# A fused transformer kernel in which both double norms and the first norm get their steps in another order

## The reference

```
def rmsnorm(x, g):
    y = x * rsqrt(mean(x * x, axis=-1) + EPS)
    return y * g

def first_block(x, ...):
    for i in range(2):
        h = rmsnorm(x, norm_mix[i])                 # n0, n2
        x = x + (forgetting_attention, retention)[i](h, ...)
        h = rmsnorm(x, norm_ffn[i])                 # n1, n3
        x = x + swiglu(h, ffn_w_in[i], ffn_w_out[i])
    return rmsnorm(x, final_norm)                   # fin

def second_block(x, ...):
    for i in range(2):
        u = rmsnorm(x, norm_pre[i])                 # n4, n5
        y = (nsa_mixer, diff_mixer)[i](u, ...)
        x = x + rmsnorm(y, norm_post[i])            # post0, post1
    return x
```

## Time and profile before

| | us |
|---|---|
| median of 3 runs | 2117.72 (2117.28 to 2118.42) |
| the profiled execution, its own time | 2117.17 |
| its span | 2115.9 |
| TensorE busy | 2051.3 (97%) |
| VectorE busy | 965.9 (46%) |
| ScalarE busy | 779.4 (37%) |
| GpSimd busy | 323.0 (15%) |

### The profile page before, as it was taken

One profiled execution on the slowest core, in us unless ns is written; L12 is line 12 of the kernel. 1 busy time (PEld: TensorE's weight loads), 2 busy tenths in 40 slices (PEclk: granted clock), 3 DMA queues, 4 the chain that ended last, 5 costly groups with the idle time before them and its releaser, 6 DMA issues. The chain is left out here.

```text
span 2115.9 us, 26709 instructions
## 1 busy us (share of the span) xinstructions
PE 2051.3 (97%) x10149; PEld 1659.6 (78%) x10149; DVE 965.9 (46%) x1967; ACT 779.4 (37%) x1557; POOL 323.0 (15%) x489
## 2 busy tenths in 40 slices
PE   7999999999999999999999999989998999899998
PEld 5887887888888886788888888867787888677766
DVE  4438434433354344435524444354435663535445
ACT  4226332222233222332322222233336884324453
POOL 2103110000002120000110000032003764402311
PEclk9999999999999999999999999999999999999999
DMA  5330232332324331132233333225321102323212
GB/s 175 101 91 19 60 123 89 92 99 90 101 69 149 100 91 50 51 99 100 79 121 91 98 100 93 90 72 181 99 70 61 32 22 100 103 80 100 70 50 80
DMA packets 96766, 187.32 MB, mean 89 GB/s; under 512 B 8407, under 2 KB 16639, under 8 KB 96512
## 3 DMA queue, kind: packets, MB, share of 16 engines
q1 hardware_dynamic: 90288, 164.35, 25.5%
q0 software_dynamic: 6352, 21.27, 3.2%
HBM read 181.33 MB, written 4.26 MB: 88 GB/s over the span
## 5 line engine op out<-in xcount | busy, mean ns | idle before, releaser
L1902 DVE TENSOR_TENSOR wl<-raw,wh 128x1024 fp32r<-128x1024 f32 x306 | 375.8, 1234 | 782.0 <-ACT wh L1352 781.1
L1352 ACT ACTIVATE wh<-raw 128x1024 fp32r<-128x1024 f32 x306 | 320.8, 1053 | 833.4 <-PE bank L729 796.8
L729 PE MATMUL bank<-hTh,wh 128*128 128x512 f32 (+2 forms) x1200 | 467.5, 390 | 0.2 <-issue 0.2
L729 PE MATMUL bank<-hTl,wh 128*128 128x512 f32 (+2 forms) x1200 | 466.9, 389 | 0.0
L729 PE MATMUL bank<-hTh,wl 128*128 128x512 f32 (+2 forms) x1200 | 466.9, 389 | 0.0
L729 PEld LDWEIGHTS bank<-hTh,wh 128*128 128x128 f32 (+2 forms) x1200 | 223.9, 187 | 48.7 <-issue 0.3
L729 PEld LDWEIGHTS bank<-hTh,wl 128*128 128x128 f32 (+2 forms) x1200 | 223.9, 187 | 48.1
L729 PEld LDWEIGHTS bank<-hTl,wh 128*128 128x128 f32 (+2 forms) x1200 | 223.9, 187 | 48.0
L729 PE MATMUL bank<-wh,hTh 128*128 128x512 f32 x400 | 156.5, 391 | 0.1
L729 PE MATMUL bank<-wh,hTl 128*128 128x512 f32 x400 | 155.7, 389 | 0.0
L729 PE MATMUL bank<-wl,hTh 128*128 128x512 f32 x400 | 155.6, 389 | 0.0
(11 more groups left out here) (368 smaller groups left out, 3105.4 us busy)
## 6 DMA issues: line engine op xcount, KB each, us to landing
raw<-in_ffn_w_in SPq DMA_DIRECT2D x88, 512.0 KB, 3.6
raw<-in_ret_w_in SPq DMA_DIRECT2D x48, 512.0 KB, 3.8
raw<-in_ffn_w_out SPq DMA_DIRECT2D x44, 512.0 KB, 3.7
raw<-in_diff_w_in SPq DMA_DIRECT2D x32, 512.0 KB, 3.7
raw<-in_fox_w_in SPq DMA_DIRECT2D x24, 512.0 KB, 3.9
raw<-in_nsa_w_in SPq DMA_DIRECT2D x20, 512.0 KB, 3.6
raw<-in_ret_w_out SPq DMA_DIRECT2D x16, 512.0 KB, 3.7
raw<-in_fox_w_out SPq DMA_DIRECT2D x8, 512.0 KB, 3.7
```

The source lines that it names most:

```text
L729: i = pe.do.matmul(dst, x, y, start=first and k == 0 and q == 0, stop=stop)
L1352: act.do.activation(M.hl[n % HL_SLOTS][0][:, 0:m], M.raw[n % RAW_SLOTS][:, 0:m], ACT.Copy).then_inc(*T.up("act_hi", n))
L1902: dve.do.tensor_tensor(wl[:, 0:m], M.raw[n % RAW_SLOTS][:, 0:m], wh[:, 0:m].bitcast(F32), ALU.subtract).then_inc(*T.up("dve_lo", n))
```

## The change

1. **SP's queue at the start:** x tile 0, gain, chunk 0, x tile 1, chunks 1, 2 and 3, x tiles 2 and 3, then the rest as before.
2. **The gain of n0** is multiplied by -0.5 by VectorE, no longer by ScalarE.
3. **ScalarE and VectorE at the start:** ScalarE splits chunk 0 between the squares of tiles 0 and 1 and chunk 1 ahead of turn 0; VectorE does the splits of chunks 0 and 1 ahead of turn 0, and scale 1 behind turn 0 and one more split.
4. **TensorE at the double norms:** D0 D1 D2 turn 0, D3, V0 with turn 1 in its middle (`turn_at=2`), V1 with turn 2 in its middle, V2 with turn 3, V3. The other norms name their turns by tile now, with the same order as before.
5. **ScalarE and VectorE at the double norms:** `act_between`, `act_final` and `dve_between` go; `act_double` and `dve_double` write the whole order out.

The number of instructions of each kind is the same, except that the one multiply of the gain moves from ScalarE to VectorE. GpSimd's program is unchanged.

```diff
+    load_x(0)
     sp.do.dma_start(M.norm["n0"][0][:, :], M.I["norm_mix"][0]...)
-    load_x(0)
+    load_weights(0)
     load_x(1)
-    load_weights(0)
-    load_weights(1)
+    for n in (1, 2, 3):
+        load_weights(n)
     load_x(2)
-    load_weights(2)
     load_x(3)
...
-                if c == 3 and late:
+                if c == turn_at and late:
...
-    pe_ffn(pe, T, M, 1, ("n3", {2: (3,)}), ("n4", 2))
+    pe_ffn(pe, T, M, 1, ("n3", {2: (3,)}), ("n4", {2: (0,)}))
...
-    pe_by_tile(pe, T, M, ["nsa v"], ..., late=("n4", {1: (2,), 2: (3,)}))
+    pe_by_tile(pe, T, M, ["nsa v"], ..., late=("n4", {0: (1,), 1: (2,), 2: (3,)}),
+               turn_at=2)
...
 def act_program(act, T, M):
-    gain = M.norm["n0"][0]
-    act.wait_ge(*T.at("ldn0", "gain"))
-    act.do.activation(gain[:, :], gain[:, :], ACT.Copy, scale=-0.5)...
...
     squares(0)
+    act_split(act, T, M)
     squares(1)
     act_split(act, T, M)
     act_turn(act, T, M, "n0", 0)
-    for _ in range(3):
-        act_split(act, T, M)
+    act_split(act, T, M)
+    act_split(act, T, M)
     squares(2)
...
+def act_double(act, T, M, post, norm, first, rest=None):
...
+    first(0)
+    rest_of(0)
+    squares(0)
+    first(1)
+    rest_of(1)
+    first(2)
+    act_turn(act, T, M, norm, 0)
+    squares(1)
+    act_split(act, T, M)
+    rest_of(2)
+    act_split(act, T, M)
+    act_split(act, T, M)
+    first(3)
+    act_turn(act, T, M, norm, 1)
+    squares(2)
+    rest_of(3)
+    act_split(act, T, M)
+    act_turn(act, T, M, norm, 2)
+    squares(3)
...
 def dve_program(dve, T, M):
-    dve_scale(dve, T, M, "n0", 0, "act_gain")
+    dve.wait_ge(*T.at("ldn0", "gain"))
+    dve.do.tensor_scalar(gain[:, :], gain[:, :], -0.5, None, ALU.mult)...
+    dve_scale(dve, T, M, "n0", 0, "dve_gain")
...
+def dve_double(dve, T, M, post, norm, first, rest):
...
+    taken(0)
+    rest(0)
+    dve_whole(dve, T, M, post, 0)
+    taken(1)
+    rest(1)
+    taken(2)
+    dve_scale(dve, T, M, norm, 0, "pool_gain")
+    dve_whole(dve, T, M, post, 1)
+    dve_turn(dve, T, M, norm, 0)
+    rest(2)
+    taken(3)
+    dve_split(dve, T, M)
+    dve_split(dve, T, M)
+    dve_scale(dve, T, M, norm, 1, "pool_gain")
+    dve_whole(dve, T, M, post, 2)
+    dve_split(dve, T, M)
+    rest(3)
+    dve_turn(dve, T, M, norm, 1)
+    dve_scale(dve, T, M, norm, 2, "pool_gain")
+    dve_whole(dve, T, M, post, 3)
+    dve_split(dve, T, M)
+    dve_turn(dve, T, M, norm, 2)
+    dve_scale(dve, T, M, norm, 3, "pool_gain")
```

More of the change, by code:

```diff
@@ L773, in pe_by_tile @@
         if closes:
-            norm, lag = closes
-            if o >= lag:
-                pe_turn(pe, T, M, norm, o - lag)
+            norm, tiles = closes
+            for t in tiles.get(o, ()):
+                pe_turn(pe, T, M, norm, t)
 def pe_by_half(pe, T, M, tag, ready, freed, late):
@@ L1547, in act_ffn, with both, final, squares @@
         a, b = (act_add_and_turn(act, T, M, "n2", f"down05 {half}", half) for half in range(2))
[L1548 to L1576 removed]
+        def both(o):
+            a(o)
+            b(o)
+        act_by_tile(act, T, M, both)
+    else:
+        def final(half):
+            return lambda t: act_squares(act, T, M, "fin", t, half, M.X[:, t, half * 512:half * 512 + 512], "dve_x", (f"down15 {half}", t))
+        act_double(act, T, M, "fin", "n4", final(0), final(1))
+    T.note("act", f"ffn{i}")
+def act_double(act, T, M, post, norm, first, rest=None):
+    def squares(t):
+        for half in range(2):
+            act_squares(act, T, M, norm, t, half, M.X[:, t, half * 512:half * 512 + 512], "dve_x", (post, t))
+    def rest_of(t):
+        if rest:
+            rest(t)
+    first(0)
[17 more added lines that the diff above has]
+    squares(3)
 def act_ret(act, T, M):
@@ L1650, in act_nsa @@
     bank = T.bank
[L1651 removed]
+    act_by_tile(act, T, M, late=("n4", {0: (3,)}))
     def take_c(o):
@@ L1917, in dve_product, with dve_by_tile @@
         dve_split(dve, T, M)
-def dve_by_tile(dve, T, M, take=None, late=None, before_last=None):
+def dve_by_tile(dve, T, M, take=None, late=None):
     for o in range(4):
@@ L2165, in dve_ffn, with both, taken @@
         a, b = (dve_add_and_scale(dve, T, M, "n2", f"down05 {half}", half) for half in range(2))
-    else:
-        a, add = (dve_add(dve, T, M, f"down15 {half}", half) for half in range(2))
-        def b(o):
-            add(o)
-            dve_between(dve, T, M, "fin", "n4", o)
-    def both(o):
-        a(o)
-        b(o)
-    dve_by_tile(dve, T, M, both, before_last=(lambda: dve_scale(dve, T, M, "n4", 2, "pool_gain")) if i else None)
-    T.note("dve", f"ffn{i}")
-def dve_between(dve, T, M, post, norm, o):
-    if o == 3:
-        while dve.held:
-            dve_release(dve, T, M)
-    if o >= 2:
-        dve_turn(dve, T, M, norm, o - 2)
-    if o in (1, 2):
-        dve_scale(dve, T, M, norm, o - 1, "pool_gain")
-    dve_whole(dve, T, M, post, o)
-    if o == 3:
-        dve_scale(dve, T, M, norm, 3, "pool_gain")
+        def both(o):
+            a(o)
+            b(o)
+        dve_by_tile(dve, T, M, both)
+    else:
+        dve_double(dve, T, M, "fin", "n4", *(dve_add(dve, T, M, f"down15 {half}", half) for half in range(2)))
+    T.note("dve", f"ffn{i}")
+def dve_double(dve, T, M, post, norm, first, rest):
+    def taken(t):
+        if first:
+            first(t)
+    taken(0)
[10 more added lines that the diff above has]
+    dve_split(dve, T, M)
+    dve_split(dve, T, M)
+    dve_scale(dve, T, M, norm, 1, "pool_gain")
+    dve_whole(dve, T, M, post, 2)
+    dve_split(dve, T, M)
+    rest(3)
+    dve_turn(dve, T, M, norm, 1)
+    dve_scale(dve, T, M, norm, 2, "pool_gain")
+    dve_whole(dve, T, M, post, 3)
+    dve_split(dve, T, M)
+    dve_turn(dve, T, M, norm, 2)
+    dve_scale(dve, T, M, norm, 3, "pool_gain")
 def dve_whole(dve, T, M, post, o):
```

64 lines of the change are left out of this document (19 added, 45 removed).

## The result

| | before | after |
|---|---|---|
| median of 4 runs each, side by side, us | 2117.93 (2117.28 to 2118.42) | 2101.98 (2100.59 to 2103.39) |
| profiled execution: own time / span, us | 2117.17 / 2115.9 | 2103.34 / 2102.0 |

The ratio is 0.9925 (95%: 0.9908 to 0.9942), so the kernel became 16 us faster. The forecast was 2102.5, range 2099 to 2109.

A forecast was written before the change was run, and what follows sets the result against it. TensorE, 97% busy, was taken as the bound, so only its waits and slow-clock time could be won. 8.0 + 5.1 + 2.1 = 15.2 us off 2117.17 gives 2102.0, plus 0.55 for the median: 2102.5, range 2099 to 2109.

The forecast's parts named there:

- nothing downstream should eat it: Outside the changed stages: TensorE is full, splits and transfers follow its releases, so the summed 15.2 us stay won.
- fin/n4: First double norm: V0 right behind D3, one 2.2 us wait before its last chunk; 8.0 us less, bounds 7.0 and 9.5.
- The favourable rival: Both double norms: GpSimd gets in between splits, outer norm 2 and split 3 come 1 to 2 us earlier; 2099, chance 0.13.
- post0/n5: Second double norm: same order and prices, a 2.1 us wait, V2 starts earlier; 5.1 us less, bounds 4.1 and 6.8.
- The start: Kernel start: first product's matmul at 14.7 instead of 16.85; 2.1 us less, 1.1 to 2.9 depending on the clock.
- the 2.9 of the working: Kernel start: the case that the clock rises 3.4 us earlier, making the start worth 2.9 us.
- The clock did not fall in the new waits: Rival, both double norms: clock falls in the 2.2 us waits, 2.4 us each; 2105 or 2107.3, chance 0.27.
- The roots did not starve VectorE: Rival, double norms: roots caught twice by VectorE instructions, 10.5 us later per stage; 2123.5, chance 0.04.
- VectorE held by GpSimd: Rival, double norms: VectorE waits for GpSimd's running step, 1.5 us per stage, 3 us; 2105.5, chance 0.03.

The follow-up runs named there:

- swap: The changed kernel with VectorE's split 3 ahead of outer norm 2 instead of behind it, in both double norms; 2102.62 us, ratio 0.993.
- gain_act: The changed kernel with the gain's multiply back on ScalarE, ahead of the squares; 2101.80 us in one execution.
- orders_only: The kernel before with only ScalarE and VectorE in the new order at the double norms, TensorE and start as before; 2103.30 us, ratio 0.9929.
- roots: The changed kernel with GpSimd's roots reordered in both double norms, outer norm 2's root before VectorE's splits 1 and 2; 2102.70 us, ratio 0.9928.
- best: The changed kernel with roots reordered in both double norms, fin 2's sum made earlier, and turn 0 ahead of split 1 at the start; 2097.06 us, ratio 0.9906.

## Why the prediction was right, point by point

The time was right (2101.98 for 2102.5), and so were the mechanisms of all three terms. That it came within 0.5 us is luck: two errors of opposite sign cancelled. The three terms were set too small by 3.1 us, and the step "nothing downstream should eat it" failed by 4.6 us in the profiled execution.

- **fin/n4: 9.2 us, predicted 8.0 (bounds 7.0 to 9.5).** The mechanism was the predicted one: V0 right behind D3, one wait for low halves ahead of its last chunk. What was mis-sized is the chain of roots. Against D0's start scale 1 came 1.0 us earlier than in the working (1412.56 with a lead of -0.27, for 1413.3), so that turn 1 had no wait instead of 0.5; outer norm 2 came 1.2 us earlier (1415.55 for 1416.5), and the wait was 1.08 us instead of 2.2. Most of this comes from further up the chain. The working had every GpSimd step beside scale 0 wait for its end, but the first step of the root of fin 1 was over before scale 0 began (1403.20 to 1403.49), the second took its 0.56 us beside it, and only the third was held up (1404.24, 0.81 us). So outer norm 1 started at 1405.50 (1405.2 against D0's start, for 1406.1), the squares of n4 1 and ScalarE's splits followed earlier (splits done at 1409.5, 1411.1 and 1412.0, for 1410.1, 1411.8 and 1412.7), and VectorE's split 2 ended at 1412.34 (1412.1, for 1413.1). Scale 1 came 0.2 us behind it, as in the working. The favourable rival, GpSimd getting in between the splits, had a small part: a step did end there (1.41 us and then 1.23, and not one step through both). In post0/n5, where one step lasted through both splits, scale 1 came 0.6 us behind split 2, so getting in was worth about 0.4 us. The gap was 0.06 us, since split 2 followed the end of its high half (2.42 us for the two splits, not 2.36). One slip of the working changes nothing in the sum: TensorE could have taken turn 1 at 1411.6 + 12 x 0.229 = 1414.35, so that the wait put at 0.5 us is 0.35 by its own numbers, and the next about 2.0.
- **post0/n5: 6.3 us, predicted 5.1 (4.1 to 6.8).** Here a step was kept out through both splits, as assumed (2.26 us). Scale 1 was still 0.4 us earlier than worked out, outer norm 2 0.7 us, and the wait was 1.27 us instead of 2.1. Between scale 1 and outer norm 2 lay 2.99 us in both stages, where the working had 3.2 and 3.3.
- **The start: 2.8 us, predicted 2.1 (1.1 to 2.9).** The first matmul came 1.85 us earlier (15.00, predicted 14.7). The rest is the clock, which rose after 7 slow matmuls at 18.12 instead of after 12 at 21.86; the 2.9 of the working (2.7 by its own figures) was that case. It is luck of the execution: `swap`, which starts alike, had 12 slow matmuls and won 2.1 us, the very case that was forecast. x tile 0 was usable at 4.31 and not at 5.3, and `gain_act` showed that most of that is lost in ScalarE's queue. The multiply of the gain took VectorE 0.69 us (estimated between 0 and 1.28). It held up the GpSimd step beside it, which took 0.93 us for 0.56, but the first product lost nothing by it, as predicted, since the early xn is not used.
- **"Nothing downstream should eat it"** is the step that failed. 18.3 us were won in the stages, 3 more than summed, and 4.6 given back in products that I had called full. They were full, but at a slower clock: the text of the prediction looked for falls of the clock only in the waits that the change makes, and not at the three waits where it already fell or could fall. That this is a matter of the execution and not of the change is shown by `swap` and by the other executions of the changed kernel: 2100.3 to 2100.6 at a mean clock of 0.995 and 2103.2 to 2103.4 at 0.993.
- **The rivals.** The clock did not fall in the new waits, which were 1.08 and 1.27 us and not 2.2; `orders_only`, with 1.97 and 2.05 us in one piece, shows the fall and its price, at most 1.7 us for 3.4 us at half speed, less than the 2.4 set down for it. That GpSimd gets in was worth some 0.4 us, in the first stage alone. The roots did not starve VectorE, though `swap` shows that one split more in the wrong place costs 1.0 us in each stage, and `roots` and `best` that a root in the wrong place of GpSimd's queue costs 2 to 4.
- **VectorE held by GpSimd.** In the double norms there is no sign of it: beside steps of GpSimd a scale or outer norm takes 1.28 to 1.31 us here, 1.28 in the earlier trace rows, and the pair of splits that began 0.13 us after a GpSimd step took 2.42 us, while the step took 1.41 instead of 0.34. The Trainium skill (SBUF — State Buffer, "SBUF: two separate sides") has whichever engine starts first hold the shared port for its whole instruction. For this pair of instructions the trace disagrees, in that the later VectorE instruction lost at most 0.06 us and the earlier GpSimd step 1.1. Beside longer GpSimd instructions the trace agrees: in the kernel before, a split that began 0.31 us after a GpSimd instruction of 1.28 us took 2.06 us instead of 1.22, and there are six lengthened splits of this kind in each of the two kernels, all outside the stages of the change.

```profile
682.02 1.28 POOL L545 TENSOR_TENSOR qr<-qr,tmp 128x512 f32<-128x512 f32 x1
682.33 2.06 DVE L1902 TENSOR_TENSOR wl<-raw,wh 128x1024 fp32r<-128x1024 f32 x1
```

So the rival was wrong for the steps of one column, and right about what a longer GpSimd instruction can do to VectorE.

Not settled: why the waits at 329, 1052 and 1596 bring a long stretch at the low clock in one execution and a short or none in another. The runs show that it varies, not what decides it. One regularity they do show: behind the wait at 329, which is 2.63 or 2.64 us long in all 13 profiled executions, the clock fell 0.2 to 0.5 us after the wait's end in six and then stayed low for 6.8 us, and 0.9 to 1.7 us after it in the other seven and stayed low for 3.4. The Trainium skill (TensorE: Matmul & The Clock Gate, "Part 1: The HAM clock gate") says that the number of slow matmuls at the start of one kernel differs from run to run; the rows agree for the rise at the start (7 slow matmuls in the changed kernel, 12 in `swap`, which starts alike) and show the same for falls in the middle of the kernel.

## What to carry to other kernels

Where a strictly ordered engine makes small results for another one, write down for each when its inputs are there, and queue them in that order: a root queued one place too early made TensorE wait 2.5 us, and the right place won 2.5 us in a stage on top of the order written by hand. A missing operand and the place where it is asked for belong together: by itself the new place of the turn took no waiting away, on top of early halves 0.9 us of it, and 3.7 us of time where the clock fell behind the wait that it cuts up. And compare a stage by the lead between its first and last matmul, not by the time of the kernel, when the kernel's time moves by 3 us with the clock.
